# A diffusion layer with RWKV-7, Hyena and PEER on one core: expert rows planned earlier, gate parts in one product, two tiles finished inside the loop, the RWKV solution summed in PSUM

## The reference, cut to what matters

```python
def layer(x, mod, s0, grid_w, p, l):
    h = rmsnorm(x, p['norm_mix'][l]) * (1 + scale1) + shift1
    m, s_fin = mixer(h, s0, grid_w, p, l)            # RWKV-7 both ways, and Hyena, then w_out
    x = x + gate1 * m
    h = rmsnorm(x, p['norm_ffn'][l]) * (1 + scale2) + shift2
    x = x + gate2 * peer(h, p, l)
    return x, s_fin

def wkv_scan(s0, r, dec, k, v, kk, kka, reverse):
    def step(s, inp):                                # 8 heads of 64
        sa = einsum('bhij,bhj->bhi', s, kk_t)
        s = s * d_t - sa[..., None] * kka_t + v_t[..., None] * k_t
        return s, einsum('bhij,bhj->bhi', s, r_t)

def peer(h, p, l):                                   # 8 heads, top 16 of 16384 experts for each token
    eidx, gate = product_key_top_k(x @ p['peer_wq'], p['peer_keys'])
    act = gelu(einsum('cd,ced->ce', x, u_tab[eidx])) * gate
    return einsum('ce,ced->cd', act, v_tab[eidx])

y_prompt, y_sample = rmsnorm(xp, final_norm), rmsnorm(xs, final_norm)   # and the final scan states
```

## Time and profile before

| | us |
|---|---|
| median of 3 timed runs | 2777.74 (2775.55 to 2778.43) |
| the profiled execution, its own time | 2768.11 |
| its span, first to last instruction | 2766.3 |
| PE busy / DVE busy | 2374.0 (86%) / 1880.2 (68%) |
| POOL busy / ACT busy | 926.9 (34%) / 426.7 (15%) |
| DMA | 638.57 MB, 231 GB/s over the span |

### The profile page before, as it was taken

How to read it: one execution, slowest core, us unless ns; L and a number is a source line. 1 busy time by engine, 2 the same in 40 slices (tenths; PEclk the granted TensorE clock), 3 DMA queues, 4 the chain that set the end, 5 groups by cost and what they waited for, 6 DMA issues and landing times.

```text
span 2766.3 us, 42661 instructions
## 1 busy us (share of the span) xinstructions
PE 2374.0 (86%) x17458; PEld 1607.1 (58%) x17458; DVE 1880.2 (68%) x3842; ACT 426.7 (15%) x831; POOL 926.9 (34%) x774
## 2 busy tenths in 40 slices
PE   5989978688788788898897289999999999998994
PEld 2545536567677674343444287776776677765552
DVE  1111255345688787675889987887899888867776
ACT  2111213123232221101111121000001000000001
POOL 0000000000023221443634003666665666665671
PEclk8999978789899998998999559999999999999997
DMA  8242130030055543667965206999998999999995
GB/s 292 92 172 72 45 108 23 24 130 2 32 173 176 162 158 118 259 238 251 334 233 178 92 5 241 381 377 380 401 379 324 409 385 387 385 380 409 409 409 205
DMA packets 195293, 638.57 MB, mean 231 GB/s; under 512 B 25158, under 2 KB 27078, under 8 KB 194138
## 3 DMA queue, kind: packets, MB, share of 16 engines
q0 software_dynamic: 110592, 402.70, 39.0%
q1 hardware_dynamic: 84506, 233.13, 22.7%
HBM read 627.11 MB, written 8.65 MB: 230 GB/s over the span
## 4 chain that ended last, share of the span: by engine, by line
PE 62%; DVE 19%; DMA 9%; issue 5%; ACT 2%; POOL 2%; SPq 1%; DVEq 0%; ACTq 0%
PE ps L1044 11%; PE ps L1055 11%; PE ps L584 7%; DMA arena<-in_peer_v,arena 6%; PE ps L1066 6%; PE ps L814 3%; PE ps L971 2%; PE ps L928 2%; PE ps L961 2%; POOL arena L2147 2%; PE ps L586 2%; DVE arena L1821 2%; PE ps L986 1%; DVE arena L1825 1%; DVE arena L1667 1%
## 5 line engine op out<-in xcount | busy, mean ns | idle before, releaser
L1055 PE MATMUL ps<-arena 128*128 128x512 f32 x1024 | 473.9, 606 | 28.7 <-DVE arena L2042 26.7
L1044 PE MATMUL ps<-arena 128*128 128x256 f32 x2048 | 478.6, 387 | 10.7 <-DMA arena<-in_uT 9.7
L2147 POOL DMA_INDIRECT arena<-in_peer_u,arena x256 | 341.3, 1333 | 335.4 <-DVE arena L1788 160.5
L1044 PEld LDWEIGHTS ps<-arena 128*128 128x128 f32 x2048 | 390.6, 194 | 80.3 <-issue 31.8
L2147 POOL DMA_INDIRECT arena<-in_peer_v,arena x256 | 307.6, 1202 | 193.9 <-DVE arena L2001 138.3
L2001 DVE SCALAR_TENSOR_TENSOR arena<-arena 128x1024 f32<-128x1024 f32 x252 | 315.5, 1284 | 73.5 <-DMA arena<-in_peer_v,arena 67.3
L2135 POOL DMA_INDIRECT arena<-in_peer_u,arena x128 | 126.4, 988 | 691.3 <-DVE arena L1788 348.9
L1055 PEld LDWEIGHTS ps<-arena 128*128 128x128 f32 x1024 | 197.2, 194 | 233.7 <-issue 225.6
L1996 DVE SCALAR_TENSOR_TENSOR arena<-arena 128x1024 bf16<-128x1024 f32 x256 | 303.8, 1222 | 39.0 <-DMA arena<-in_peer_u,arena 34.0
L1066 PEld LDWEIGHTS ps<-arena 128*128 128x128 bf16 x3072 | 207.3, 157 | 52.8 <-issue 47.2
L814 PE MATMUL ps<-arena 64*64 64x128 f32 x1920 | 188.1, 285 | 40.9 <-DVE arena L1861 33.3
(11 more groups left out here) (351 smaller groups left out, 3306.7 us busy)
## 6 DMA issues: line engine op xcount, KB each, us to landing
arena<-in_uT SPq DMA_DIRECT2D x128, 512.0 KB
arena<-in_peer_v SPq DMA_DIRECT2D x128, 512.0 KB
arena<-in_w_ada SPq DMA_DIRECT2D x12, 2048.0 KB, 11.5
arena<-in_peer_wq SPq DMA_DIRECT2D x8, 2048.0 KB, 9.3
arena<-in_w_in SPq DMA_DIRECT2D x6, 2048.0 KB, 8.0
arena<-in_w_out SPq DMA_DIRECT2D x4, 2048.0 KB, 7.9
arena<-in_peer_u,arena POOLq DMA_INDIRECT x384
arena<-in_peer_v,arena POOLq DMA_INDIRECT x384
```

Source lines behind the costliest of these rows:

```text
L1044: m = pe.matmul(ps[:, 4 + i % 2, 0:ND], us[i % UB][:, k, :], hTd[:, k, :], start=(k == 0), stop=(k == KD - 1))
L1055: m = pe.matmul(ps[:, 2 * r + c, :], sgel[:, i % SBUFS, P * r:P * r + P], vs[i % VB][:, 512 * c:512 * c + 512], start=(i == 0), stop=(i == ...
L2147: pool.indirect_dma_start(gring[:, n % RING, :], None, a[("peer_u", "peer_v")[e]][0], bass.IndirectOffsetOnAxis(ap=ids[:, t, m:m + 1], axi ...
```

## The change

Five things change.
- `rows_by`: 400 of the 512 rows come in tiles 9 to 95, 4.6 a tile, the other 112 in tiles 96 to 126, 3.6 a tile. Tile 1 is routed over tiles 0 to 7, tile 2 over 40 to 55.
- `one_hots`: the three products of the equality with the three parts of the gate become one product of 768 elements into a buffer of its own, the equality is kept in `same_i`.
- The finish is cut into `fin_sum`, `fin_mean` and `fin_norm` (ACT: `fin_square`, `fin_root`). Tiles 0 and 1 are finished at tiles 104 to 106 and 108 to 110 of the loop; x and the norm weight are loaded by SP at tile 100. Tile 2 follows the last rows, and tiles 3 and 4 are interleaved.
- In the solve x stays in PSUM: at the first level PE adds it with an identity (`i64`), and all levels accumulate. DVE's addition is gone, ACT copies x to SBUF after each step, 12 copies a unit, ahead of the copy of N.
- `PREP_ACT` and `PREP_DVE` place the pieces of preparation after other steps.

```diff
 def rows_by(i):
-    return max(0, min(ROWS, (i - 5) * ROWS // (ETILES - 8)))
+    return max(0, min(EARLY, (i - 8) * EARLY // 87)) + max(0, min(ROWS - EARLY, (i - 95) * (ROWS - EARLY) // 31))
...
-ROUTE_STEPS = {1: (0, 5), 2: (40, 52)}
-FIN_ORDER = (0, 1, 3, 4, 2)
+ROUTE_STEPS = {1: (0, 8), 2: (40, 56)}
+FIN_AT = {104: 0, 108: 1}
...
-PREP_ACT = {0: 1, 1: 1, 4: 1, 5: 2, 6: 1, 8: 1, 9: 2, 10: 1}
-PREP_DVE = {0: 2, 3: 2, 4: 3, 5: 2, 6: 1}
+PREP_ACT = {1: 1, 2: 1, 4: 1, 5: 2, 7: 1, 8: 1, 9: 1, 10: 1, 11: 1}
+PREP_DVE = {2: 2, 3: 2, 4: 3, 5: 2, 6: 1}
...
@@ SP, in the loop over tiles
-            sp.wait_ge(S("a_ok"), ETILES)
-            sp.dma_start(xr, spill).then_inc(S("ld_xr"), 16)
-            sp.dma_start(fnorm, a["final_norm"].partition_broadcast(P)).then_inc(S("ld_xr"), 16)
+                if i == 100:
...
+                    sp.wait_ge(S("a_ok"), (NPART - 1) * QI)
+                    sp.dma_start(xr, spill).then_inc(S("ld_xr"), 16)
+                    sp.dma_start(fnorm, a["final_norm"].partition_broadcast(P)).then_inc(S("ld_xr"), 16)
...
@@ PE, the doubling
+                            if l == 0:
+                                for r in (low, high):
+                                    pe.matmul(xo[r, u, :, i, :], i64[r, :], zz[r, h // 2, 0:2, i, :], start=(j == 0), stop=False,
+                                              skip_group_check=True)
                             for r in (low, high):
-                                m = pe.matmul(xo[r, u, :, i, :], nT[r, :], zz[r, h // 2, 0:2, i, :], start=True, stop=True)
+                                m = pe.matmul(xo[r, u, :, i, :], nT[r, :], zz[r, h // 2, 0:2, i, :], start=False, stop=(l == LEVELS - 1),
+                                              skip_group_check=True)
...
@@ ACT, the doubling
+                        act.wait_ge(S("r_lv"), 12 * n + 2 * l + g + 1)
+                        own.do(A(zz[:, 2 * g:2 * g + 2, 0:2, :, :].rearrange("p u k i j -> p u (k i j)"),
+                                 ps[:, 1 + 3 * g, :].rearrange("p (u x) -> p u x", u=2), ACT.Copy), S("r_lvx"))
                         if l < LEVELS - 1:
-                            act.wait_ge(S("r_lv"), 12 * n + 2 * l + g + 1)
...
@@ ACT, the loop over tiles
+                if i in FIN_AT:
+                    fin_square(FIN_AT[i])
+                if i - 1 in FIN_AT:
+                    fin_root(FIN_AT[i - 1])
+            fin_square(2)
+            fin_root(2)
+            fin_square(3)
+            fin_square(4)
+            fin_root(3)
+            fin_root(4)
...
@@ DVE, the doubling
-                        dve.wait_ge(S("r_lv"), 12 * n + 2 * l + g + 1)
-                        if l == 0 and g == 0:
-                            dve.wait_ge(S("r_x0"), 2 * n + 2)
-                        xg = zz[:, 2 * g:2 * g + 2, 0:2, :, :].rearrange("p u k i j -> p u (k i j)")
-                        own.do(V.tensor_tensor(xg, ps[:, 1 + 3 * g, :].rearrange("p (u x) -> p u x", u=2), xg, ALU.add), S("r_lvx"))
...
@@ DVE, one_hots
-                rown.do(V.tensor_tensor(oi[:, 2, :, :], iota8[:, 0, QI * q:QI * q + QI, :], col(0, QI), ALU.is_equal))
                 V.tensor_tensor(one_j[:, g % 2, :, :], iota8[:, 0, :, :], col(1, P), ALU.is_equal)
+                if g >= 1:
+                    dve.wait_ge(S("one_ok"), g)
+                rown.do(V.tensor_tensor(same_i[:, 0, :, :], iota8[:, 0, QI * q:QI * q + QI, :], col(0, QI), ALU.is_equal))
                 rown.settle()
-                for k in range(2):
-                    m = V.tensor_tensor(oi[:, k, :, :], oi[:, 2, :, :], col(2 + k, QI), ALU.mult)
-                rown.do(m)
-                rown.settle()
-                V.tensor_tensor(oi[:, 2, :, :], oi[:, 2, :, :], col(4, QI), ALU.mult).then_inc(S("one_ok"), 1)
+                V.tensor_tensor(one_i[g % 2], same_i.to_broadcast([P, 3, QI, GRP]),
+                                slot5[:, 2:5, d, c:c + GRP].unsqueeze(2).to_broadcast([P, 3, QI, GRP]), ALU.mult).then_inc(S("one_ok"), 1)
...
@@ DVE, the loop over tiles
+                if i in FIN_AT:
+                    fin_sum(FIN_AT[i])
+                if i - 1 in FIN_AT:
+                    fin_mean(FIN_AT[i - 1])
+                if i - 2 in FIN_AT:
+                    fin_norm(FIN_AT[i - 2])
...
-                        for _ in range(66 // (hi - lo)):
+                        for _ in range(64 // (hi - lo)):
...
-            for k in range(2):
-                finish(k)
-            for k in range(2, NT):
-                finish(k)
+            fin_sum(2)
+            fin_mean(2)
+            fin_norm(2)
+            fin_sum(3)
+            fin_sum(4)
+            fin_mean(3)
+            fin_mean(4)
+            fin_norm(3)
+            fin_norm(4)
```

46 lines of the change are left out of this document (25 added, 21 removed).

## The result

The changed kernel takes 2740.3 us (median of four runs, 2737.8 to 2745.4) where the kernel before takes 2776.6 beside it: a ratio of 0.988, 95% interval 0.986 to 0.990. It is faster by 36 us, half of what was forecast, and just outside the range. The profiled execution took 2737.8 us, its span 2736.0, 30.3 less than before. By stage, each between the same instructions of both traces: tail -21.0, loop -6.8, gate groups -1.1, solve -2.0, what lies between +0.5.

A forecast was written before the change was run, and what follows sets the result against it. PE bounds three quarters of the expert loop, DMA the fourth; solve and tail come next. Gains of 23 (tail), 22 (loop), 2 (gate groups) and 22 (solve) sum to 69 us: 2777.7 to 2709 us, range 2690 to 2738 for 8 in 10.

The forecast's parts named there:

- Forecast 12.9 us: Tail, PE's last matmul to the end: 35.9 us falls to 12.9, a gain of 23.
- 22 us of gain: Expert loop: PE would end near 2709 us instead of 2730.4; at most 39 us could be gained.
- the stall of the second, taken at 9: Loop's second quarter: six long DVE routing passes still fall into two tiles, so the stall of 9 us stays.
- of which 5 to 10 are covered by what is ahead: Loop's fourth quarter: of 17 us DMA excess, rows already ahead cover 5 to 10, leaving 9 to 10 of waiting.
- those 6.3 us and the lead: Loop: each quarter's end without gate groups takes back 6.3 us; eight row buffers (10 us) and one tile bound the lead.
- the early rate does not hold: Rival, loop's first 87 tiles: queues give only 384 GB/s, not 404, so the loop ends about 22 us later, 2731; chance 0.13.
- The load of x does stall PE: Rival, fourth quarter: x holds up `peer_v` loads, PE stalls 5 to 8 us at `back`; 2709 to 2715, within the forecast's 0.60.
- the 2 us of the forecast: Gate groups before the loop: 32 groups save about 0.05 us each, 2 us in all.
- gains nothing: Rival, RWKV solve: PE's wait moves from DVE to ACT and the added matmuls are bare; 2731 us, chance 0.15.
- the 18 that were counted: Solve: PE's 16 added identity matmuls a unit cost 1.8 us, 18 in all.
- a plain unit comes to 27.7 + 1.8 + about 0.5 = 30: Solve: a unit with gathered rows and no routing falls from 32.4 us to 30, 2.5 to 3 less.
- the sum has 15: Solve: the five plain units together were entered at 15 us in the solve's gain of 22.

The follow-up runs named there:

- after_again: The changed kernel once more, unaltered, as a base line and second profile: 2726.3 us, 0.987 of the kernel before.
- after_third: The changed kernel a third time, unaltered, as a base line: 2730.1 us, 0.989 of the kernel before.
- solve_back: Changed kernel with the old RWKV solve: DVE adds x, no identity matmuls or ACT copies of x, old preparation tables; 2730.0 us, 0.988 of the kernel before.
- even_rows: Changed kernel with the 512 rows spread evenly over tiles 9 to 126, 4.34 a tile: 2750.8 us, 0.995 of the kernel before.
- start_early: Changed kernel with rows begun at tile 6, 414 by tile 95, tile 2 routed over tiles 36 to 53: 2711.8 us, 0.979 of the kernel before.
- early_x_split: `start_early` with 410 early rows, x and the norm weight loaded in six pieces at tiles 100 to 118: 2709.6 us, 0.980 of the kernel before.
- experiment 2: Changed kernel without the 320 identity matmuls that add x into PSUM (output not the reference's): 2713.9 us, 0.982 of the kernel before.
- experiment 4: Changed kernel, context rows moved: all beside doubling steps, 2768.3 us; one a unit in units 4 to 9, 2835.3; ten a unit, none in rest stretches, 2758.5.
- fill: Changed kernel with 8 and 14 useless matmuls where PE waits at a unit's end in the solve: 2723.0 us, 0.985 of the kernel before.

## Why the prediction was half right

**Tail: right.** Forecast 12.9 us, measured 15.0, and 12.2 to 13.5 in the other kernels with this tail. In the first profile the root's table load stands bare ahead of tile 2's norm:

```profile
2720.90 1.28 ACT L1389 ACT_TABLE_LOAD   x1
...
2722.43 0.16 DVE L2086 RECIPROCAL arena<-arena 128x1 f32<-128x1 f32 x1 [1.36 <-ACT arena L1389]
```

**Loop: mechanism right, three terms too small.** The forecast had 22 us of gain. Measured were 7 in the first profile and 8 to 10 in `after_again`, `after_third` and `solve_back`, which share the loop. The first and third quarter at 272 came out at 273 to 275, 3 to 4 us in all; the stall of the second, taken at 9, at 10 to 13, and 17 in the first profile; the fourth, taken at 223, at 226 to 228. That last step reads "of which 5 to 10 are covered by what is ahead": by bytes it is 31 x (2 + 3.6) x 0.524 / 0.409 + 7.7 = 230 us, so only 3 to 4 us were covered. What was ahead had been spent: in the last tiles of the third quarter without groups, DVE's lead over PE (from its weighing to `back`) fell from 11 us (tile 89; 7 in `after_again`) to 1 us (tile 96). The forecast counted those 6.3 us and the lead, and didn't subtract one from the other. The arithmetic of bytes came within 5 us in all four plans: 230 for 226 to 228 here, 259.5 for 259.3 in `even_rows`, 213 for 215.6 in `start_early` and, with 102 late rows, 218 for 213.2 in `early_x_split`.

The rival "the early rate does not hold" fell: the third quarter moved 399 GB/s and took 273 to 275 us. The reading against it, that DVE waited there for PE and not for DMA, was half true. In the third quarter before, DVE waited 30.1 us for PE and 20 us for the DMAs of its rows.

The load of x does stall PE, by 6 us and a block at half clock, but the place was wrong: not at `back` for its `peer_v`, but through the rows, which share the bytes and which DVE was waiting for anyway. x took 13.7 us to land and the norm weight, sent behind it, 16.3, the issues below, where I had taken 10 from the earlier trace rows. By the Trainium skill's rule in DMA: Bandwidth & Descriptors, section "Queues, rings and completion order", that the queues take turns, the estimate was 15. The trace agrees, within 2 us.

```profile
arena<-x_spill SPq DMA_DIRECT2D x1, 2560.0 KB, 13.7
...
arena<-in_final_norm SPq DMA_DIRECT2D x1, 512.0 KB, 16.3
```

**Gate groups: right.** The product of 768 elements takes 558 ns, forecast 0.55 us, so the repeated operand keeps the fast rate. The Trainium skill's rule in VectorE: DVE Perf Modes, section "What auto-detection actually checks", that 16-bit operands of step 1 get two elements a cycle, would have it so, and the trace agrees. The matmuls of the 32 groups before the loop took 53.2 us from first to last instead of 55.2, the 2 us of the forecast; up to the loop's first `back` 1.1 of them were left.

```profile
L2054 DVE TENSOR_TENSOR arena<-arena 128x768 bf16<-128x768 bf16 x101 | 56.3, 558 | 3.5
```

**Solve: wrong, the rival "gains nothing" holds, but not for its reason.** ACT was hardly late. PE's waits between 740 and 1040 us, before, then after:

```profile
PE ps L814 <- DVE arena L1861: 18.2, 15, 1.9
...
PE ps L832 <- DVE arena L1861: 5.1, 5, 1.0
```

```profile
PE ps L841 <- ACT arena L1205: 5.3, 3, 2.3
PE ps L822 <- ACT arena L1281: 4.2, 5, 0.9
...
PE ps L841 <- ACT arena L1278: 2.0, 2, 1.1
```

23 us of waits for DVE became 12 for ACT (8 in `after_again`). The identity matmuls cost the 18 that were counted (experiment 2), and the routing unit gave its 8. What failed is the step "a plain unit comes to 27.7 + 1.8 + about 0.5 = 30". Its base was the unit of the earlier trace rows, which has the clock at 1.00; the five plain units before are 34.4, 34.0, 32.3, 34.0 and 32.4 us, three of them with a slow start, and after they are 30.5 at clock 1.00 and 32 to 33 otherwise, and mostly otherwise. At equal clock the change is thus worth 1.9 us a plain unit, 32.4 to 30.5, near the 2.4 of the forecast's working. But the five took 163 us on average over eight profiles (159 to 167) and 167 before, a gain of 4, where the sum has 15. That 15 was too large by itself: 32.4 - 30 is 2.4, five times 12. The second omission is the rest stretches, priced at nothing: 103 to 107 us for five, 100 before, and 100 again once the gathered rows are out (experiment 4). In sum the stage took 606.1 us on average over the eight profiles, against 607.9 over the two with the old solve: -2 us against -22.

Why the half clock is so often there after the change, when PE's waits at a unit's end are much the same as before, is not settled. That the half clock follows from these waits is shown by `fill`. Over the whole stage the clock is 0.92 before and in `after_again` alike.

## To carry to other kernels

When a wait is taken off an engine, its queue runs ahead until something else stops it: here DVE ran into the DMAs of its gathered rows, and moving more rows into the freed time made the kernel 1% slower. Price a pipelined stage from all its instances, with the clock beside each, not from the best one. Where a stretch is bound by bytes, count them and believe the sum to within a few us; a lead that a formula gives you must be followed to the place where it is used, and what was used on the way subtracted. In this kernel the waits of PE between phases cost twice, once themselves and once in the half clock behind them.

## What the runs showed of the hardware

Much of what differs between runs of the same solve is TensorE's clock: the same code took 597.7 to 611.8 us, and its plain units 30.5 at clock 1.00, 32.1 at 0.95 and 33 at 0.93. Useless matmuls in a wait of 1.3 and one of 2.1 us kept the granted clock of the rest stretches at 1.00, where it was 0.81 to 0.92 in 31 of 40 without them. Bulk loads, tile loads and gathered rows together reached 409 GB/s in the changed kernel, and 409 to 413 in the fastest slice of each of the twenty profiles. A load of 3.1 MB beside a saturated stream of rows landed in 16.7 us, and DVE waited 4.9 us for one of the rows.
